# The start addresses of the activation buffers of a two-block transformer kernel: 32 bytes past a multiple of 128

## What is computed

```python
def first_block(x, ...):                      # cut
    h = rmsnorm(x, norm1_gain)
    (aq, ak, av, mq, mk, mv, mi, mf, mo, gate_a, gate_m) = split_columns(h @ w_in)
    att_b = sliding_window_attention(rope(norm(aq)), rope(norm(ak)), av, sinks) @ w_branch_attn
    hm = mlstm_chunkwise(mq, mk, mv, i_pre, f_pre)
    ml_b = (rmsnorm(hm) * sigmoid(mo)) @ w_branch_mlstm
    x = x + (sigmoid(gate_a) * att_b + sigmoid(gate_m) * ml_b) @ w_out
    return x + peer_ffn(rmsnorm(x, norm2_gain), ...)   # 8 heads x 16 experts of 16384 per token

def second_block(x, ...):                     # cut
    q, k, v, q_hg, f_hg, i_hg, g_hg, gate_sb, gate_hg = split(rms_norm(x) @ w_in_2)
    y_sb = stick_breaking_attention(norm(q), norm(k), v) @ w_branch_2[:512]
    y_hg = hgrn2_mixer(q_hg, f_hg, i_hg, g_hg, ...) @ w_branch_2[512:]
    h = x + (sigmoid(gate_sb) * y_sb + sigmoid(gate_hg) * y_hg) @ w_out_2
    hn = rms_norm(h)
    return h + (silu(hn @ w_gate) * (hn @ w_up)) @ w_down
```

## The kernel before

| tensor | start before | after | start mod 128 before | after |
|---|---|---|---|---|
| ring, rows_w | 16,512 | 16,512 | 0 | 0 |
| w_hi | 49,280 | 49,280 | 0 | 0 |
| w_lo | 65,664 | 65,664 | 0 | 0 |
| xres | 82,048 | 82,048 | 0 | 0 |
| hT_lo, xn | 90,240 | 90,272 | 0 | 32 |
| hT_hi | 98,432 | 98,464 | 0 | 32 |
| arena | 106,624 | 106,752 | 0 | 0 |

## Time and profile before

### The profile page before, as it was taken

How to read it: one execution, slowest core, us unless ns; L and a number is a source line. 1 busy time by engine, 2 the same in 40 slices (tenths; PEclk the granted TensorE clock), 3 DMA queues, 4 the chain that set the end, 5 groups by cost and what they waited for, 6 DMA issues and landing times.

```text
span 1324.2 us, 16101 instructions
## 1 busy us (share of the span) xinstructions
PE 1178.5 (89%) x6088; PEld 840.0 (63%) x6088; DVE 715.8 (54%) x1452; ACT 577.7 (44%) x1269; POOL 845.9 (64%) x511
## 2 busy tenths in 40 slices
PE   7999999978987787788678777788999999999999
PEld 7987999973332333333233333333889999999998
DVE  5443154389776675857768576555789623311111
ACT  7486564434323222324322222224676375644442
POOL 7696578776645454444554445442987558788885
PEclk9999999999989998988998998899999999999999
DMA  8443446469999999999999999998543336555542
GB/s 270 147 160 127 138 166 207 159 259 426 425 426 425 426 425 426 426 425 427 425 425 426 426 425 426 427 425 329 185 164 127 126 126 196 167 191 184 186 159 96
DMA packets 130221, 381.81 MB, mean 288 GB/s; under 512 B 8544, under 2 KB 83296, under 8 KB 97376
## 3 DMA queue, kind: packets, MB, share of 16 engines
q0 software_dynamic: 36864, 268.45, 48.3%
q1 hardware_dynamic: 91808, 112.25, 25.4%
q10 hardware_dynamic: 1472, 0.09, 0.1%
HBM read 379.72 MB, written 1.05 MB: 288 GB/s over the span
## 4 chain that ended last, share of the span: by engine, by line
PE 57%; DMA 31%; DVE 7%; ACT 2%; POOL 2%; issue 1%; SPq 0%; DVEq 0%; ACTq 0%
PE ps L694 30%; DMA rows_w<-peer_rows_in,arena 30%; PE ps L967 9%; PE ps L723 6%; PE ps L1139 4%; DVE rows_w L2122 2%; PE ps L1092 2%; POOL rows_w L653 1%; PE ps L1041 1%; DMA ring<-w_in_in 1%; DVE arena L2122 1%; ACT wgt L1460 1%; PE ps L784 0%; PE ps L759 0%; PE ps L770 0%
## 5 line engine op out<-in xcount | busy, mean ns | idle before, releaser
L465 POOL TENSOR_TENSOR w_lo<-ring,w_hi 128x1024 fp32r<-128x1024 f32 x204 | 503.2, 2485 | 142.7 <-ACT w_hi L449 142.5
L967 PE MATMUL ps<-arena,diag 128*128 128x512 f32 x448 | 222.2, 646 | 85.3 <-ACT diag L1469 85.3
L967 PE MATMUL ps<-rows_w,diag 128*128 128x512 f32 x508 | 244.3, 630 | 33.6 <-ACT diag L1469 33.6
L449 ACT ACTIVATE w_hi<-ring 128x1024 fp32r<-128x1024 f32 x204 | 209.9, 1057 | 137.2 <-PE ps L694 98.6
L653 POOL DMA_INDIRECT arena<-peer_rows_in,arena x112 | 131.3, 1172 | 171.9 <-PE ps L967 156.6
L694 PE MATMUL ps<-hT_hi,w_hi 128*128 128x256 f32 x816 | 234.4, 287 | 3.7 <-POOL w_lo L465 3.7
L653 POOL DMA_INDIRECT rows_w<-peer_rows_in,arena x128 | 165.8, 1295 | 109.6 <-PE ps L967 96.6
L694 PE MATMUL ps<-hT_lo,w_hi 128*128 128x256 f32 x816 | 231.5, 284 | 0.0
L694 PE MATMUL ps<-hT_hi,w_lo 128*128 128x256 f32 x816 | 231.4, 284 | 0.0
L967 PEld LDWEIGHTS ps<-arena,diag 128*128 128x128 f32 x448 | 87.6, 203 | 215.8 <-ACT diag L1469 120.2
L2122 DVE CUSTOM_DVE_ANT_0 rows_w<-rows_w,arena 128x1024 f32<-128x1024 f32 x128 | 155.4, 1224 | 106.8 <-DMA rows_w<-peer_rows_in,arena 106.6
(11 more groups left out here) (419 smaller groups left out, 1743.2 us busy)
## 6 DMA issues: line engine op xcount, KB each, us to landing
ring<-w_in_in SPq DMA_DIRECT2D x45, 1024.0 KB, 5.0
ring<-w_ffn_gate_in SPq DMA_DIRECT2D x11, 1024.0 KB, 5.1
ring<-w_ffn_up_in SPq DMA_DIRECT2D x11, 1024.0 KB, 5.2
ring<-w_ffn_down_in SPq DMA_DIRECT2D x11, 1024.0 KB, 5.0
ring<-w_out_in SPq DMA_DIRECT2D x8, 1024.0 KB, 5.3
ring<-w_branch_attn_in SPq DMA_DIRECT2D x4, 1024.0 KB, 5.9
ring<-w_branch_mlstm_in SPq DMA_DIRECT2D x4, 1024.0 KB, 5.3
ring<-peer_w_query_in SPq DMA_DIRECT2D x4, 1024.0 KB, 5.3
```

Source lines behind the costliest of these rows:

```text
L449: act.activation(hi_of(n, u)[:, t, 0:cols], raw_half(n, g)[:, t, 0:cols], ACT.Copy).then_inc(sem("hi_ready"), 1)
L465: pool.tensor_tensor(lo_of(n, u)[:, t, 0:cols], raw_half(n, g)[:, t, 0:cols], hi_of(n, u)[:, t, 0:cols].bitcast(F32), ALU.subtract).then_i ...
L967: ins = pe.matmul(acc[:, c, :], diag[:, p % 4, :], pick_row(p % TOPK, D + c * CW, CW), start=False, stop=True, skip_group_check=True)
```

## The change

The change touches only where tensors and views start; no instruction is added, removed or moved on any engine.

```diff
         xres = sb("xres", [P, NB, D])
+        freq = sb("freq", [P, RH])
         with ExitStack() as shared:
             xn = shared.enter_context(nc.sbuf_tensor("xn", [P, NB, D], F32))
         hT_lo = sb("hT_lo", [P, KT, S], R32)
         hT_hi = sb("hT_hi", [P, KT, S], R32)
+        sinks = sb("sinks", [P, AH])
+        mlgain = sb("mlgain", [P, KT])
...
-        hmT_lo = Area(at_mva).take(KT, S, dt=R32)
+        hmT_lo = Area(at_mva + 16).take(KT, S, dt=R32)
...
-        x3w_hi = at(12288, KT, P, dt=R32)
-        x3w_lo = at(13312, KT, P, dt=R32)
+        x3w_hi = at(12264, KT, P, dt=R32)
+        x3w_lo = at(13288, KT, P, dt=R32)
...
-        osbT_hi = at(3072, SBW // P, S, dt=R32)
-        osbT_lo = at(16384, SBW // P, S, dt=R32)
+        osbT_hi = at(3080, SBW // P, S, dt=R32)
+        osbT_lo = at(16392, SBW // P, S, dt=R32)
...
-        ohgT_hi = at(5120, HGW // P, S, dt=R32)
-        ohgT_lo = at(6144, HGW // P, S, dt=R32)
+        ohgT_hi = at(5128, HGW // P, S, dt=R32)
+        ohgT_lo = at(6152, HGW // P, S, dt=R32)
...
-        rbc = at(17408, S)
+        rbc = at(17416, S)
...
-        mixT2_hi = at(10240, KT, S, dt=R32)
-        mixT2_lo = at(12288, KT, S, dt=R32)
+        mixT2_hi = at(10248, KT, S, dt=R32)
+        mixT2_lo = at(12296, KT, S, dt=R32)
         silu = at(3072, 2, 2, S)
-        hidden = Area(3072 + 1024)
+        hidden = Area(3072 + 1032)
```

More of the change, by code:

```diff
@@ L154, in build @@
         gcol = sb("gcol", [P, 4, KT])
-        mlgain = sb("mlgain", [P, KT])
         qkgain = sb("qkgain", [P, 2, ROPE])
@@ L158, in build @@
         turn = sb("turn", [P, 4, 2, NB, RH])
-        sinks = sb("sinks", [P, AH])
         ifbias = sb("ifbias", [P, 2, MH])
         pos_i = sb("pos_i", [P, NB], I32)
-        freq = sb("freq", [P, RH])
         ss = sb("ss", [P, NB])
```

## The result

The forecast was 1316.0 us. The changed kernel takes 1329.18 us (median of 8 runs, 1328.10 to 1330.88), the one before, in as many runs beside it, 1325.88 (1323.98 to 1326.99): a ratio of 1.0026, interval 1.0017 to 1.0035. So it is slower by a little more than what can be told from no change. The profiled execution has a span of 1327.3 us; before it had 1324.2.

The account below looks back on a forecast made before the run. TensorE's own stream was taken to bound the dense products, DMA the experts' stage. Savings of 7.2 + 0.6 + 1.0 = 8.8 us from 1324.2, plus 0.5 for the median and 0.1 lost, gave 1316.0 us; range 1312.0 to 1325.0.

Parts of the forecast that it names:

- moving, 256 columns: Dense products streaming `hT`, `osbT` or `ohgT`: 2554 matmuls on the chain save 2.8 ns each, 7.2 us.
- held, 256 columns: Dense products holding `hT` or `mixT2` while weights stream: 365 matmuls save 1.6 ns each, 0.6 us.
- wide: Matmuls with 512 columns, holding `hT`, `x3w` or `arena` activations: 602 save 1.6 ns each, 1.0 us.
- `attT`, `hmT`, `mixT`: First-block products with starts already apart: `attT` and `mixT` unchanged though `arena` moved by 128, `hmT` nearer to 117.2 ns.
- gather: Transfers of expert rows in the experts' stage: rate still 422 GB/s, 0 us difference in that part.
- first chunk: First weight chunk's 96 matmuls: half come to equal starts and lose 2.8 ns each, 0.1 us slower.
- In the gather nothing of this matters: Experts' stage: the moved starts leave the gather's time alone; the stage only begins and ends earlier.
- the rival with the slower rows in `arena`: Gather rows moved to 128 past a multiple of 256 are written slower: 4.4 us more, 1320.4; chance 0.04.
- What the distance saves comes out of this fixed part: Matmuls with 512 columns: savings come from 12.7 ns per matmul independent of columns, so 1.6 ns each.
- No wait on POOL: Dense products: POOL covers the faster TensorE; its 1.0 us wait could double, PE's waits staying under some 10 us.
- The row in `xn`: Gather target moved to 32 past a multiple of 64: writes might take twice as long, 40 us, 1356; chance 0.07.
- no effect: Dense products: shorter pitches belong to their place in the program, not the address; time 1324.7, chance 0.12.

Follow-up runs that it names:

- e5_rows0: Kernel before, everything from `rows_w` on 128 bytes later and the rows in `arena` another 128, so all sixteen rows stand at multiples of 256: 1324.56 us, ratio 0.9984.
- e4_rows128: Kernel before with only the seven expert rows in `arena` starting 128 bytes later; no operand of a product moves: 1331.65 us, ratio 1.0041.
- e9_after_rows0: The changed kernel with the seven expert rows in `arena` put back to multiples of 256: 1323.34 us, ratio 0.9973 of the kernel before.
- e1_arena128: Kernel before with only `arena` moved, by 128 bytes; `xn`, `hT` and the views in `arena` stay: 1334.10 us, ratio 1.0065.
- e2_ht32: Kernel before with only `hT` and `xn` moved by 32 bytes; `arena` keeps its place modulo 256: 1321.07 us, ratio 0.9957.
- e7_probe: Separate program of matmuls alone, activations at eight distances from the weights: moving with 256 columns 113.3 to 120.1 ns, held with 512 columns 226.7 to 234.1.
- e3_ht32_xn0: Kernel before with `hT` moved by 32 bytes, `xn` left in place and `arena` moved by 256: 1320.38 us, ratio 0.9955.
- e8_dist192: Kernel before with all rows at multiples of 256 and nearly all narrow products' activations at distance 192, `hidden` and `x3w` at 0: 1314.62 us, ratio 0.9909.
- e6_best: Kernel before with all rows at multiples of 256, `hT`, `osbT`, `ohgT`, `mixT2` at distance 32, `hidden` and `x3w` at 0: 1317.54 us, ratio 0.9932.

## Why the prediction was wrong

Its reading that the starts of the operands move the time of a matmul was right, though not that one distance has one time. Three other places outweighed what it brought. The terms on the chain, in us:

| term | predicted | measured | how |
|---|---|---|---|
| moving, 256 columns | -7.2 | -7.6 | 2362 x 3.1 ns (3.2 in the second block, 2.8 in the first), and line 1092's 192 x 1.3 |
| held, 256 columns | -0.6 | -0.3 | 182 of `hT` x 1.6 (119.9 to 118.3); `mixT2` nothing |
| wide | -1.0 | +3.3 | 338 of line 723 x 5.2, 264 of lines 1139 and 1123 x 6.0 |
| `attT`, `hmT`, `mixT` | 0 | +0.95 | 46.09 - 45.33 in the x384 piece, some 0.2 ahead of it |
| gather | 0 | +7.2 | between the marks |
| first chunk | +0.1 | not told apart | |
| sum | -8.7 | +3.6 | the spans say +3.1, the medians +3.3 |

The measured terms of the matmuls are pitches of the traces times the prediction's counts, so they are estimates. With 1 to 2 us between traces of one program, the sum agreeing so closely is in part luck.

**The gather** is the step that turned the sign. "In the gather nothing of this matters" stood in the sum, and the rival with the slower rows in `arena` had a chance of 0.04 and a price of 4.4 us, as if only the moved rows paid. It was set aside because the rows in `rows_w`, odd already, land in 27.1 us and those in `arena` in 27.0. That was the wrong row. By the times to landing about eleven transfers are under way, so these times hold mostly the transfers ahead. The 29.0 us of `xn`, which the prediction put down to its start at 128, are no sign of a start either: with `xn` at a multiple of 256 (`e5_rows0`) they are 29.0 again. A packet's own time would have been a warning: the old trace already had 313 ns against 309 at rows 13 to 15. `e4_rows128` shows the cause alone (1.0041), `e9_after_rows0` that taking it away gives the gain back. The mechanism differs from the rival's too: its cut-off part of 1.6% would be paid by every odd row, and odd rows with fewer than three odd ones ahead pay nothing. And rows 6 and 7 in `rows_w`, which did not move, went from 309 to 313.5 ns.

**The wide matmuls.** "What the distance saves comes out of this fixed part", so a wide one would save as much as a narrow held one: that was argued, from no row, and bounded by 0 and 3.3 ns of gain. It is a loss of 5 to 6 ns. The prediction said itself that no row shows 512 columns with the starts apart; with no row the bounds should have been open to both sides. `e1_arena128` and `e2_ht32` show the loss, 5 ns each, and the probe: 6 to 7 ns at every distance but 0 and 192, and 2 at 192.

**`attT`, `hmT` and `mixT`.** The first and the last were to stay and `hmT` to gain, since 128 was taken for the period. The rows at hand had no pair of starts that differ by 128, so the period was a guess. It is longer: 118.7 ns at 128 against 120.0 at 0, narrow, and 232.8 against 226.7, wide. By `arena`'s 128 bytes `mixT2` came from 0 to 160, which for a held one is 120.0 as well. `mixT` came from 32 to 160, 118.3 to 120.0 by the probe and 118.4 to 120.0 in the kernel, and line 1092's activations from 0 to 160, 118.7 by the probe and 118.8 in the kernel. `attT`'s and `hmT`'s 120.0 ns are 1.3 more than the probe has at 160.

**What was right.** `hT` moving at 32: 116.7 where 117.2 was said (the probe has 117.8, and some pieces of the kernel too; rows 4 already had both pitches for `attT`, and the prediction averaged them). No wait on POOL took the place. The row in `xn`, feared at 0.07, costs nothing (`e2_ht32` against `e3_ht32_xn0`). And "no effect", that the pitch belongs to the place in the program, is refuted by `e3_ht32_xn0` and by the probe: the last stage's `hT` went from 119.9 to 116.7 ns where little but its start changed.

## What to carry to other kernels

Where a start is moved, list all that stands in or behind that buffer, the targets of transfers too, and price each. Here the moved starts gained about 8 us on the narrow products and lost about 11 on the wide ones, on the buffers in `arena` and in the gather. In a queue that is full, compare the time of the packets, not the time to landing, which is mostly the queue's. A rate of transfers that is the bound of a stage for half of the span deserves a bound of its own in every prediction: 1% of it turned the sign of the whole effect. And where rows at one distance show two pitches, as `attT`'s did (117.8 and 116.7), the distance is not the only cause; look for both before taking the mean.

## What the runs showed of the hardware that was not expected

- In a stream of weight loads and matmuls of fp32r, one with 256 columns takes 113.3 to 120.1 ns and one with 512 takes 226.7 to 234.1, at eight distances of the two operands' starts with nothing else running (`e7_probe`). Of a move from 0 to 32 narrow ones gained where wide ones lost.
- At one distance several pitches appear in one kernel: 113.6 and 117.8 ns at 192 (`e8_dist192`), 116.7, 117.8 and 120.0 at 32 (`e6_best`). What chooses is open.
- A gather of rows of 8192 bytes moves 427 GB/s with all its places at multiples of 256, 426 with seven even and nine odd, and 421 with all of them odd. Packets take 309.1, 310.1 and 313.5 ns. In the mixture the slow ones are those with at least three odd rows directly ahead. That one row, `xn`'s, stands 32 past an odd place costs nothing that can be seen (`e2_ht32`, `e3_ht32_xn0`).
